# Seven block products in a split-precision SwiGLU: the weight splits are grouped anew and two products and one addition change their place

## The reference, cut to what matters

```
def swiglu(h, w_gu, w_down):
    gu = h @ w_gu
    g, u = gu[..., :D_FF], gu[..., D_FF:]
    return (jax.nn.silu(g) * u) @ w_down
```

## Time and profile before

| what | value |
|---|---|
| median of 3 runs | 3064.26 us (3059.1 to 3067.65) |
| profiled execution: own time, span | 3066.81 us, 3065.0 us |
| TensorE matmuls busy | 2822.1 us, 92% of the span |
| VectorE busy | 2099.3 us, 68% |
| ScalarE busy | 1232.7 us, 40% |
| GpSimd busy | 543.9 us, 18% |
| mean granted TensorE clock | 0.973 of full |
| read from HBM | 238.34 MB, 78 GB/s |

### The profile page before, as it was taken

The page is one execution under the profiler, slowest core; times in us unless marked ns, Lnnn a source line. Parts: engine busy times, 40 slices in busy tenths (PEclk is TensorE's granted clock), DMA queues, the critical chain, the costliest instruction groups (busy, mean ns, idle before and its releaser), DMA issues.

```text
span 3065.0 us, 48078 instructions
## 1 busy us (share of the span) xinstructions
PE 2822.1 (92%) x18638; PEld 2371.5 (77%) x18638; DVE 2099.3 (68%) x2856; ACT 1232.7 (40%) x1975; POOL 543.9 (18%) x371
## 2 busy tenths in 40 slices
PE   9888999998888998889999988899999999988888
PEld 7777886777788877878767777887878666878787
DVE  6777656567777667776655777776666876577775
ACT  4333445453333543334454433345344212433334
POOL 1222012011111112210210222110101431122111
PEclk9999999999999999999999999999999999999999
DMA  4222221122222322222211322222210231321212
GB/s 145 78 77 86 78 105 50 42 96 75 80 86 76 103 86 70 84 85 80 90 37 64 114 69 86 86 96 80 76 37 25 86 92 36 109 86 68 78 70 96
DMA packets 57006, 242.38 MB, mean 79 GB/s; under 512 B 6472, under 2 KB 10888, under 8 KB 38048
## 3 DMA queue, kind: packets, MB, share of 16 engines
q1 hardware_dynamic: 54896, 233.51, 22.2%
q10 hardware_dynamic: 1568, 6.64, 0.6%
q0 software_dynamic: 400, 0.23, 0.0%
HBM read 238.34 MB, written 2.10 MB: 78 GB/s over the span
## 4 chain that ended last, share of the span: by engine, by line
PE 63%; DVE 15%; DMA 8%; issue 7%; ACT 5%; POOL 2%; SPq 1%; DVEq 0%; POOLq 0%; ACTq 0%
PE psum L655 62%; DMA ring<-in_wgu 6%; DVE scr_r L2363 6%; DVE ring_lo L2363 2%; POOL ring L3407 2%; DVE highs L2363 1%; ACT highs L1876 1%; ACT highs L1860 1%; PE psum L1185 1%; DMA ring<-in_wd 1%; DVE hid_r L2363 1%; DVE ring L2475 1%; ACT highs L1842 1%; ACT highs L1833 1%; SPq L685 1%
## 5 line engine op out<-in xcount | busy, mean ns | idle before, releaser
L655 PE MATMUL psum<-highs 128*128 128x512 f32 (+2 forms) x3560 | 1177.8, 361 | 112.8 <-DVE scr L2508 102.3
L655 PEld LDWEIGHTS psum<-highs 128*128 128x128 f32 x3560 | 693.8, 198 | 241.7 <-DVE scr L2508 127.6
L655 PE MATMUL psum<-h_lo,highs 128*128 128x256 f32 (+1 forms) x2200 | 713.9, 325 | 0.0
L655 PE MATMUL psum<-highs,ring_lo 128*128 128x512 f32 (+1 forms) x1272 | 474.9, 388 | 0.0
L655 PEld LDWEIGHTS psum<-h_lo,highs 128*128 128x128 f32 x2200 | 431.4, 196 | 29.2 <-issue 0.5
L3407 POOL TENSOR_TENSOR ring<-ring 128x512 f32<-128x512 f32 x90 | 141.6, 1573 | 1291.3 <-DMA ring<-in_wgu 699.9
L2363 DVE TENSOR_TENSOR ring_lo<-ring,highs 128x1024 fp32r<-128x1024 f32 (+3 forms) x173 | 268.0, 1550 | 106.3 <-ACT highs L1751 60.8
L655 PEld LDWEIGHTS psum<-highs,ring_lo 128*128 128x128 f32 x1272 | 238.1, 187 | 50.5 <-issue 0.5
L655 PE MATMUL psum<-scr_r,highs 128*128 128x256 f32 (+1 forms) x752 | 164.4, 313 | 106.3 <-DVE scr_r L2363 99.3
L2363 DVE TENSOR_TENSOR wdr_lo<-wdr,highs 128x512 fp32r<-128x512 f32 x110 | 126.6, 1151 | 196.5 <-ACT highs L1833 196.5
L1837 ACT ACTIVATE scr<-scr 128x512 f32<-128x512 f32 x110 | 69.5, 631 | 446.4 <-DVE scr L2522 424.1
(11 more groups left out here) (463 smaller groups left out, 5578.5 us busy)
## 6 DMA issues: line engine op xcount, KB each, us to landing
ring<-in_wgu SPq DMA_DIRECT2D x105, 1024.0 KB, 5.1
wdr<-in_wd SPq DMA_DIRECT2D x110, 256.0 KB, 2.6
ring<-in_wd SPq DMA_DIRECT2D x25, 1024.0 KB, 4.8
ring<-in_wmix SPq DMA_DIRECT2D x28, 512.0 KB, 3.6
ring<-in_wmix SPq DMA_DIRECT2D x12, 1024.0 KB, 5.2
ring<-in_wproj SPq DMA_DIRECT2D x22, 512.0 KB, 3.6
ring<-in_wmix SPq DMA_DIRECT2D x8, 768.0 KB, 4.4
ring<-in_wgu SPq DMA_DIRECT2D x10, 512.0 KB, 6.0
```

Of the source, the lines that this page charges most:

```text
L655: return nc.tensor.matmul(o, w, r, start=start, stop=stop, skip_group_check=True)
```

## The change

The three groups of splits are cut in another way. The sums stay a group of two, but their high parts move to the other half of `gu_hi`. The tops now have columns 0 to 1535 (a11, a12 and s3), and their low parts go to the larger tile `scr_r`. The rests have only columns 1536 to 2559 (a22 and s4), with their low parts in `hid_r`. So the high tops wait for GpSimd's second sum, which the high rests waited for before, and for the end of s3 of the block before (`done_count(.., 5)` in the place of 4).

On TensorE a22 comes ahead of s4, but for the last block; the wait for the rests moves from s3 to behind `down1`, and a12 waits for all four readings of the block before.

The lists become, for the period of block j:

- ScalarE: high rests(j), silu(j-1), u1, high hid(j-1), u2, high sums(j+1), high w_down(j), u3, high tops(j+1).
- VectorE: gate_second(j-1) with its scaling, low rests(j), inner(j-1), low hid(j-1), sum2(j+1), sum4(j+1), gate_first(j), low sums(j+1), low w_down(j), up_second(j), low tops(j+1), the scaling of the up half, up_first(j).

Number, size and arithmetic of all products and sums stay. GpSimd's and SyncE's code isn't changed.

```
-        tops_lo = hid_r[:, 22:24, :].rearrange("p a b -> p (a b)")
-        rests_lo = scr_r[:, 4608:6144]
+        tops_lo = scr_r[:, 4608:6144]
+        rests_lo = hid_r[:, 22:24, :].rearrange("p a b -> p (a b)")
...
                     else:
                         pe.wait_ge(ring_split, blocks_split(n0, j, 2))
-                        pe.wait_ge(gu_read, read_count(f, j, -4))
+                        pe.wait_ge(gu_read, read_count(f, j, -5))
...
                     if not first:
-                        pe.wait_ge(gu_read, read_count(f, j, -1))
+                        pe.wait_ge(gu_read, read_count(f, j, 0))
                     block_product(G, a12, h21, True).then_inc(gu_done, 1)
                     pe.wait_ge(u_put, put_count(f, j, 2))
-                    pe.wait_ge(ring_split, blocks_split(n0, j, 3))
...
                     down1(j - 1, 1 - s, f, o, False, False, (0, 1, 2) if last else (0, 1, 2, 3))
-                    pe.wait_ge(gu_read, read_count(f, j, 2))
-                    block_product(Q, s4, h22, False).then_inc(gu_done, 1)
-                    pe.wait_ge(u_put, put_count(f, j, 3))
-                    if first:
-                        pe.wait_ge(h_split, h_splits(i) + 12)
-                    block_product(R, a22, r4, False).then_inc(ring_free, 1)
+                    pe.wait_ge(ring_split, blocks_split(n0, j, 3))
+
+                    def fourth():
+                        pe.wait_ge(u_put, put_count(f, j, 3))
+                        if first:
+                            pe.wait_ge(h_split, h_splits(i) + 12)
+                        return block_product(R, a22, r4, False)
+
+                    def third():
+                        pe.wait_ge(gu_read, read_count(f, j, 2))
+                        return block_product(Q, s4, h22, False)
+
                     if last:
+                        third().then_inc(gu_done, 1)
+                        fourth().then_inc(ring_free, 1)
                         down1(j - 1, 1 - s, f, o, False, False, (3,))
+                    else:
+                        fourth().then_inc(gu_done, 1)
+                        third().then_inc(ring_free, 1)
...
                 def high_tops(j, s, first=False):
...
-                    act.wait_ge(ring_in[sl], landed(n0 + PLAIN + s) + 8 * (j - s - PLAIN))
+                    act.wait_ge(s_made, sum_count(f, j, 2))
                     if not first:
-                        act.wait_ge(gu_done, done_count(f, j - 1, 4))
-                    nc.scalar.activation(gu_hi[:, par, 0:1024], ring[:, sl, 0:1024], ACT.Copy).then_inc(ring_high, 1)
+                        act.wait_ge(gu_done, done_count(f, j - 1, 5))
+                    nc.scalar.activation(gu_hi[:, par, 0:1536], ring[:, sl, 0:1536], ACT.Copy).then_inc(ring_high, 1)
...
                 def high_rests(j, s):
...
                     act.wait_ge(ring_free, used(n0 + j - 1))
-                    act.wait_ge(s_made, sum_count(f, j, 2))
                     act.wait_ge(s_put, sum_count(f, j, 2))
-                    nc.scalar.activation(gu_hi[:, 1 - par, 512:2048], ring[:, sl, 1024:2560], ACT.Copy).then_inc(ring_high, 1)
+                    nc.scalar.activation(gu_hi[:, 1 - par, 1024:2048], ring[:, sl, 1536:2560], ACT.Copy).then_inc(ring_high, 1)
...
-                    low(rests_lo, ring[:, (s + par) % 2, 1024:2560], gu_hi[:, 1 - par, 512:2048].bitcast(F32), ring_split)
+                    low(rests_lo, ring[:, (s + par) % 2, 1536:2560], gu_hi[:, 1 - par, 1024:2048].bitcast(F32), ring_split)
```

More of the change, by code:

```diff
@@ L927, in swiglu @@
                 hi, hi2 = gu_hi[:, par, :], gu_hi[:, 1 - par, :]
-                a11, a12 = ((hi[:, c], tops_lo[:, c]) for c in (slice(0, 512), slice(512, 1024)))
-                s1, s2 = (hi[:, 1024:1536], sums_lo[:, 0, :]), (hi[:, 1536:2048], sums_lo[:, 1, :])
-                s3, a22, s4 = ((hi2[:, 512 + c:1024 + c], rests_lo[:, c:c + 512]) for c in (0, 512, 1024))
+                a11, a12, s3 = ((hi[:, c:c + 512], tops_lo[:, c:c + 512]) for c in (0, 512, 1024))
+                s1, s2 = (hi2[:, 0:512], sums_lo[:, 0, :]), (hi2[:, 512:1024], sums_lo[:, 1, :])
+                a22, s4 = ((hi2[:, 1024 + c:1536 + c], rests_lo[:, c:c + 512]) for c in (0, 512))
                 def part(first, tokens):
@@ L1886, in period @@
                     r = b + 3 * s
+                    high_rests(j, s)
                     silu(j - 1, 1 - s)
-                    high_rests(j, s)
                     put_u(u1, r, j, 1, None if first else -3, 1)
                     high_hid(j - 1, 1 - s)
-                    high_wd(j, s)
                     if first:
-                        act.wait_ge(ring_free, used(n0 + PLAIN - 1))
                         high_t(t4_hi, blocks(t4), 4)
-                    put_u(u2, r, j, 3, None if first else -1, 2)
+                    put_u(u2, r, j, 3, None if first else 0, 2)
                     if not last:
                         high_sums(j + 1)
+                    high_wd(j, s)
+                    put_u(u3, r, j, 5, None, 3)
+                    if not last:
                         high_tops(j + 1, 1 - s)
                     else:
-                        act.wait_ge(gu_done, done_count(f, j, 4))
                         split_ring(n0 + NJ, gu_hi[:, par, :], DOWN_COLS[0])
-                    put_u(u3, r, j, 5, None, 3)
                 next_ring(0)
@@ L1921, in swiglu @@
                 high_hid(2, 0)
+                high_wd(3, 1)
                 high_tops(PLAIN, 0, True)
-                high_wd(3, 1)
+                act.wait_ge(ring_free, used(n0 + PLAIN - 1))
                 high_sums(PLAIN)
@@ L2487, in low_sums @@
                     dve.wait_ge(s_put, sum_count(f, j, 2))
-                    into = gu_hi[:, par, 1024:2048].rearrange("p (a c) -> p a c", a=2)
+                    into = gu_hi[:, 1 - par, 0:1024].rearrange("p (a c) -> p a c", a=2)
                     low(sums_lo, sums, into.bitcast(F32), ring_split)
@@ L2492, in low_tops, with weight_sums, up_first @@
                     dve.wait_ge(ring_high, blocks_split(n0, j, 1 if first else 2))
-                    low(tops_lo, ring[:, (s + par) % 2, 0:1024], gu_hi[:, par, 0:1024].bitcast(F32), ring_split)
+                    low(tops_lo, ring[:, (s + par) % 2, 0:1536], gu_hi[:, par, 0:1536].bitcast(F32), ring_split)
                 def low_rests(j, s):
                     dve.wait_ge(ring_high, blocks_split(n0, j, 3))
-                    low(rests_lo, ring[:, (s + par) % 2, 1024:2560], gu_hi[:, 1 - par, 512:2048].bitcast(F32), ring_split)
-                def up_first(j, s):
-                    dve.wait_ge(ring_free, used(n0 + j))
+                    low(rests_lo, ring[:, (s + par) % 2, 1536:2560], gu_hi[:, 1 - par, 1024:2048].bitcast(F32), ring_split)
+                def weight_sums(j, s, first=False):
+                    sum2(j, s, first)
+                    sum4(j, s)
+                def up_first(j, s, last=False):
+                    if last:
+                        dve.wait_ge(ring_free, used(n0 + j))
+                    else:
+                        dve.wait_ge(gu_done, done_count(f, j, 6))
                     nc.vector.tensor_tensor(up_r[:, A_TOK], psum[:, b + 3 * s, A_TOK], rms_r[:, A_TOK], ALU.mult).then_inc(gu_read, 1)
-                    dve.wait_ge(gu_read, read_count(f, j, 4))
                 def up_second(j, s):
@@ L2508, in up_second, with up_second_scaled @@
                     nc.vector.tensor_tensor(up_r[:, B_TOK], psum[:, b + 1 + s, A_TOK], u3, ALU.add).then_inc(gu_read, 1)
+                def up_second_scaled(j, s):
                     dve.wait_ge(gu_read, read_count(f, j, 2))
@@ L2515, in gate_first, with gate_second @@
                     nc.vector.tensor_tensor(probs[:, s, A_TOK], psum[:, b + 2 - s, A_TOK], u1, ALU.add).then_inc(gu_read, 1)
-                def gate_second(j, s):
-                    dve.wait_ge(gu_done, done_count(f, j, 6))
+                def gate_second(j, s, last=False):
+                    if last:
+                        dve.wait_ge(gu_done, done_count(f, j, 6))
+                    else:
+                        dve.wait_ge(ring_free, used(n0 + j))
                     nc.vector.tensor_tensor(probs[:, s, B_TOK], psum[:, b + 1 + s, A_TOK], u2, ALU.add).then_inc(gu_read, 1)
-                    dve.wait_ge(gu_read, read_count(f, j, 3))
+                    dve.wait_ge(gu_read, read_count(f, j, 3 if last else 4))
                     nc.vector.tensor_tensor(probs[:, s, :], probs[:, s, :], rms_r, ALU.mult).then_inc(gate_scaled, 1)
@@ L2527, in period @@
                     else:
-                        up_first(j - 1, 1 - s)
+                        gate_second(j - 1, 1 - s)
+                    low_rests(j, s)
                     inner(j - 1, 1 - s)
-                    low_wd(j, s)
-                    low_rests(j, s)
                     low_hid(j - 1, 1 - s)
@@ L2535, in period @@
                     if not last:
-                        sum2(j + 1, 1 - s)
```

(18 more changed lines are left out.)

2 lines of the change are left out of this document (1 added, 1 removed).

## The result

The changed kernel takes 2775.52 us (median of 4 runs, 2774.58 to 2776.26), the kernel before 3065.74 us (4 runs): ratio 0.9057, 95% interval [0.9041, 0.9072]. 2816 us was forecast, so it saved 290 us where 250 were expected. In later runs the kernel before took 3056.3 to 3082.9 us (11 runs, median 3069.1).

What follows compares the result with a forecast made beforehand. TensorE was held up by VectorE's late up_second and low rests, and the clock behind these waits. 3066.8 less 235 (85 periods) less 13 (edges) gave 2819, or 2816 us against the runs' median; range 2770 to 2920.

Steps and rivals of the forecast that it cites:

- What bounded the kernel: Blocked periods: 13.3 us TensorE work, 2.1 waits for up_second and low rests from VectorE, 0.8 slower clock: 16.2.
- The timetable: One blocked period over all engines: no wait queued ahead of TensorE; smallest slack 1.1 us, low tops before a11.
- The first lock: On VectorE, low hid held up beside GpSimd's first sum, ending 11.3 us after the previous s3's end.
- The period: Blocked periods fall from 16.16 to 13.4 us, 85 times: 235 us saved.
- Rival A: The forecast itself: TensorE sets the blocked period, 13.0 to 14.1 us, total 2770 to 2884; chance 0.62.
- The 0.1 for late weights: Added to the mean blocked period for late landings, which eat the slack before a11; 0.1 us.
- The clock: In the blocked stretches, 0.8 us a period lost behind waits is given back; at 0.95 the saving is 175 us.
- The edges: First blocked periods: 2.6 us saved, 5 times, 13 us in all; last block taken at nothing.
- the direct products of block 3 cover it: First blocked period: block 4's high tops wait for GpSimd, 2.6 us after landing, without holding up TensorE.
- B: Blocked loop: VectorE's own chain sets the period at 14.5 us, total 2910; chance 0.24.
- C: Blocked loop: the wait only moves from s3 to a11, period about 16 us, total 3064; chance 0.05.
- D: Blocked loop: GpSimd's second sum delays the low tops, a11 stalls 2.5 us, total 3101; chance 0.09.

Runs made afterwards that it cites:

- run 5: The kernel before with u3 ahead of the high tops on ScalarE and up_second ahead of the low tops on VectorE: 2980.0 us in one run.
- run 11: The kernel before with all four weight sums on VectorE, none on GpSimd, and nothing else changed: 3035.7 us in one run.
- run 8: The changed kernel with all four weight sums on VectorE ahead of sum2, none on GpSimd: 2753.0 us in one run.
- run 1: The changed kernel with up_second behind the low tops again on VectorE: 2864.4 us in one run.
- Run 10: The changed kernel with block 4's tops split early for columns 0 to 1023, the last 512 after GpSimd's second sum: 2770.8 us (4 runs).

## Why the prediction was right

**What bounded the kernel: right.** Two waits for VectorE's list and the clock behind them. Runs 5 and 11 show more than the text said: the two waits hang together. Where the lock is gone (run 11), the wait for the rests vanishes and the one for `up_second` takes over most of it. Where `up_second` is treated at its place (run 5), its wait shrinks by half, the other stays, and 86 us are gained: they are coupled, but not one and the same. Of the kernels run here, only those with the whole set of new lists let go of both.

**The timetable: right in its order, with about a microsecond less slack where weights are late.** In the late block above, measured from s3's end (145.19): `up_second` at 3.9 (timetable 3.2), low tops at 5.6 (4.9), with a11 due at 5.6 (6.0). The slack of 1.1 was 0.0 in this block. Over 80 blocks a11 started 0.06 to 1.1 us after the end of the low tops, 0.7 in the median. The first lock didn't happen here (low hid at 141.96 took 0.69, as GpSimd began at 142.18); the later landing set sum2 in its place. That case was in the text, with 0.2 left.

**The period: the term that was mis-sized is TensorE's own work.** 13.31 us were taken; it is 12.83. The down product was read as 3.10 us, from 160.44 to 163.54; after the change it takes 2.75 (145.19 to 147.94), where nothing waits. The row held a wait that no list names: low hid, locked, ran from 158.78 for 1.78 us, to 160.56, so that the down product's first matmul came at 160.71, 0.27 late, and 0.08 more went on its first matmuls. That is 0.35. In the kernel before, 59 of the 85 down products in these stretches start 0.1 to 0.3 us late (whether for low hid each time is not shown), and after the change none. Rival A of the forecast took the better figure, 2.8, from the block before. A product is 1.44 (143.75 to 145.19), not 1.46: 0.13 for seven.

The 0.1 for late weights had the right size: in 27 of 80 periods a11 starts 0.1 to 0.2 us late, too little to stand among the waits, and the period of 12.96 is 0.13 above TensorE's own 12.83. In run 8, where GpSimd makes no sums, it is one a11 in 80, so that lateness alone doesn't do it. So 13.4 - 0.35 - 0.13 = 12.92, against 12.96 measured. That the sum for before closed at 16.2 was luck: the waits and the slower clock took some 3.4 us of 16.27, not 2.9, and TensorE's own work half a microsecond less.

**The clock: right.** 1.00 in all stretches. Had it stayed at 0.95, the period would have been 13.5 at 12.83 of work. The runs say more: with 90 waits of 0.84 us on the mean (run 1) the clock of the span was still 0.995; with waits of up to 2.8 us (run 5) 0.982; with 85 of 2.0 us on the mean (run 11) 0.965. It also goes with the spread of the kernel before: of its 11 later runs the shortest, 3056.3 us, had 0.977 and the longest, 3082.9 us, 0.965. The Trainium skill ("TensorE: Matmul & The Clock Gate", Part 1) has it follow how busy the engine has been, and these figures agree.

**The edges: right in sum, wrong in one step.** Outside the `up_second` stretches only 3 us were saved (1691.0, which is 3065.0 - 1374.0, to 1687.9), where 13 were given; but 7 us of a22 have moved there, as said above. By TensorE's marks the 80 periods were forecast to save 80 x 2.76 = 221 us and saved 264.8; the five first periods and the edges were forecast to save 5 x 2.76 + 13 = 27, and saved 25.8. The step that failed is "the direct products of block 3 cover it". They don't: the high tops of block 4 now stand behind both of GpSimd's sums, and a11 waits, 2.4 us in the first layer, with the clock at 0.62 for 3 us behind it, and 0.9 to 1.0 in the others, with the clock at 1.00. This was made up for in part: 2.5 us of wait were expected to stay in the first blocked period, and 1.3 to 1.5 did. TensorE's row and the window in the first layer:
```profile
66.80 0.39 PE L655 MATMUL psum<-highs 128*128 128x256 f32 x1 [2.39 <-DVE scr_r L2372]
```
```profile
66.80:69.80 3.00, 3.00 (x15) 2.81 (x16) 2.97 (x4) 1.06 (x3) 0.00 (x0) 0.62 0.00 0
```
The wait of 3.89 us before s4 became two short ones, 0.8 before a22 and 0.5 before s4. Run 10, without the new wait, saved 8.5 us more outside the 80 periods (1729.4 us) and lost 3.8 in them.

**The rivals.** B (VectorE's loop sets the period) didn't come true, but it stood near: of 0.61 us more work ahead of `up_second` 0.25 came through. C and D: apart from the first blocked period, a11 waits 0.2 us at the most. VectorE was busy for 10.84 us of a period, not 11.8, since it lost less time to GpSimd: the split of 1536 columns took 2.52 us on the mean before and 1.76 after, low w_down 1.15 (126.6 us over 110) and 0.69 (76.3); sum2 went the other way, from 0.91 to 1.66.

## What to carry to other kernels

Lay one period of a loop out as a timetable over all engines, with what is needed when, before touching a list; two waits for the same in-order engine can hang together, so that treating one of them moves it (102.3 and 99.3 us became 169.9 and nothing in run 11). Take the busy engine's own work from a stretch where nothing at all waits, and look behind each small gap for an instruction that ends just then, since the floor decides how much there is to gain. Measure a loop between marks that enclose the same work before and after: the `up_second` marks moved 7 us of a22 out of the loop and made a right forecast of the edges look wrong. When a change has two halves, run each without the other: here the new lists with the old groups were as fast as the whole, once u2 had its place (the new groups with the old lists were not run). Work given to a helper engine isn't free if the two shut each other out: here GpSimd's two sums cost VectorE as much time as making them itself, and TensorE waited longer for what hangs on them.

## What the runs showed of the hardware that was not expected

GpSimd's additions and VectorE's of two SBUF inputs take turns whole, and neither gains. sum2 took 1.78 us (median of 90) beside GpSimd's second sum and 0.68 alone, in the same place of the same list. In 80 of the 90 blocks GpSimd's sum had started first, and sum2 ended 0.55 us after it every time; in the other 10 sum2 had started first, took 0.69, and GpSimd's sum took 1.8 for 1.3. And with both of GpSimd's sums (0.69 us each on VectorE, 1.30 and 1.62 on GpSimd) moved over, VectorE's busy time stayed the same (921.5 and 921.0 us) and the kernel became 0.8% faster. The Trainium skill ("GPSIMD Engine Reference", 8. Key points) states that GpSimd shares its SBUF interfaces with VectorE, with contention at two SBUF inputs; the trace agrees. That the later one waits out the whole instruction, and what this comes to in a loop, the runs show.
